# Token-column norm sums with a spread factor, and four reorderings taken back, in a three-layer fp32 block kernel

## The chip, the cores and the metric

The kernel runs on one core of a Trainium2 chip. The metric is the device time of one execution in microseconds, lower is better. All data are fp32; a matrix product is made of three products of rounded halves (high times low, high times high, low times high), so that each weight block costs three passes of TensorE.

## The reference, cut to what matters

256 tokens of width 1024 and 256 context tokens go through two layers of a first kind, then one layer of a second kind. All multiplications by weights are right products with 1024-wide inputs.

```python
def rms_norm(x, g):
    return x * rsqrt(mean(x * x, -1) + 1e-6) * g

for l in range(2):                         # first_block
    sh, sc, gt = modulation(c, ada_w[l], ada_b[l])
    h  = rms_norm(x,  norm_pre[l]) * (1 + sc) + sh
    hc = rms_norm(xc, norm_pre[l]) * (1 + scc) + shc
    z, zc = h @ w_in[l], hc @ w_in[l]      # in the last layer zc: keys and values only
    # differential attention, a long convolution, a gated MLP: y_a, y_b, y_c
    out = sum(sigmoid(z_sel_i) * ((y_i * silu(z_gate_i)) @ w_branch[l][i])) @ w_out[l]
    x   = x + gt * rms_norm(out, norm_post[l])
# second block, one layer
h = rms_norm_2(x, g_mix)                   # attention heads with rotary angles cos/sin(pos * inv_freq),
...                                        # compressed keys and values, a gated FFN, a last projection
```

## The kernel before, in words

x is kept transposed, as eight feature tiles of 128 x tokens. The weights come as one stream of 364 tiles (512 KB each, 128 x 1024 floats), in the order of use. Five engines run programs that are written out by hand and meet only in semaphores; within an engine the order of the program is the order of the work.

- SyncE (line 2707) requests a tile into one of four raw buffers once DVE has split the tile four places before (for a tile of the modulation, called ada, that is used raw: once TensorE has used it).
- ACT rounds the raw tile to its high half `whi` (act_hi, line 1271), in act_tiles three tiles ahead of the tile that it evacuates. DVE subtracts it for the low half `wlo` (dve_lo, line 1813), in dve_tiles two tiles ahead. `split=False` means that an iteration does its evacuation and no split, because one was done earlier.
- TensorE takes, per tile, eight blocks of 128 x 128, each with three products into one of four PSUM banks, `G` (lines 424 to 426).

The norms: ACT squares each feature tile (line 1255), TensorE adds the squares over the partitions by a product with a constant matrix `mean_all` (128 x 128), which leaves every partition of a 128 x 256 bank with the mean of each token; ACT takes the root (line 1259), DVE the reciprocal (line 1805), 128 x 256 each, and DVE multiplies. For the norm of `out` POOL first adds up seven of the eight squares (line 2660, pe_pooled line 636).

Layer 1 of the first kind uses the tiles 132 to 135 (queries), 136 to 139 (ada), 140 to 143 (keys), then values, convolution, MLP and gates up to 191, the terms and selectors 192 to 215 (the sum over the branches), and w_out 216 to 223. The second block begins with 224 and 225 (called zc), 226 to 228 (heads), 229 to 232 (compressed keys); later come down (332 to 353), pproj (354, 355) and pgate (356 to 363).

- pe_cross (from line 801) is the start of layer 1: the sums of the norm of x, three ada tiles, the four query tiles (pe_cross_queries, line 764, in the order QUAD, which has two or three tiles interleaved block by block as the halves of h arrive), and the fourth ada tile, 139, behind the sixth step of that order. ACT's read of the ada sums is line 1402; it stands in act_beside, ahead of h(4).
- w_out: in iteration o of eight, each engine does one tile. DVE also works out a part of the arguments of the rotary angles in o = 0 to 3 (dve_trig, line 2064: cosine in two parts, sine in two parts), and ACT applies Sin at o = 2 and 4 (line 1648). At o = 5 ACT makes a root of one column, which loads its Sqrt table early (line 1645).
- Behind w_out: the norm of out (on PE, `("out", 1)`), then eight stages x = x + factor * out (lines 2435 and 2436, semaphore x_new), each followed by ACT's square for the norm `("res", 1)`. DVE makes one extra split ahead of the first and one behind the last, ACT one rounding behind the root.
- POOL waits for x_new(1, 7), then issues the copies head_spread, ck_w2, cv_w2 (lines 2686 to 2688), because their place is in use until then. pe_block2 (line 1131) waits for the three, then for the factor of the norm, and begins with pe_mix_quad (line 1017), in which the tiles 224 to 227 are interleaved in the order QUAD as the halves hn(k) arrive.
- In the down loop DVE and POOL add the results to x and the squares for the next norm; DVE splits tile 356 in its iteration i == 4.

Of the kernel before, what the change touches and what calls it, by code (L numbers as in the profile page):

```python
# [10 lines left out]
ACT = mybir.ActivationFunctionType  # L11
# [215 lines left out]
class Kernel:  # L227
# [407 lines left out]

    def pe_pooled(self, stage, n):

        bank = self.sum_bank.get(stage, self.M[0])[:, 0:n]
# [125 lines left out]
    def pe_cross_queries(self, tiles, last_ada):  # L764

        n = 0
        for step, (i, k) in enumerate(QUAD):
# [10 lines left out]
            if step == 5:  # L778
                self.pe_tile(last_ada)
# [20 lines left out]
    def pe_cross(self):  # L800
# [4 lines left out]
        for T in moving[:3]:  # L805
            self.pe_tile(T)
        self.pe_cross_queries(queries, moving[3])
# [163 lines left out]
    def pe_block1(self, l):  # L971
# [35 lines left out]
        self.pe.wait_ge(*self.at("rstd", ("out", l)))  # L1007
        for k in range(KT):
            self.pe_sum(("res", l), k, n)
# [6 lines left out]

    def pe_mix_quad(self):

        pe, n = self.pe, 0
        tiles = self.tiles[self.pe_next:self.pe_next + 4]  # L1020
        for i, k in QUAD:
            T = tiles[i]
            s, c = T.t % SPLIT, slice(k * P, (k + 1) * P)
            if k == 0:
                pe.wait_ge(*self.at("tile_lo", T.t))
                self.pe_bank(T.use)
            if k == n:
                pe.wait_ge(*self.at("hn", "g_mix", k))
                n += 1
            m = self.three(self.G[T.use % 4][:, 0:TOK], self.whi[:, s, c], self.wlo[:, s, c], self.hi(k, 0), self.lo(k, 0), k == 0, k == KT - 1)  # L1030
            if k == KT - 1:
                m.then_inc(*self.mark("tile_used", "used", T.t))
        self.pe_next += 4
# [97 lines left out]
    def pe_block2(self):  # L1131
# [5 lines left out]
        pe.wait_ge(*self.at("rstd", ("res", 1)))  # L1137
        self.pe_mix_quad()
        self.pe_tiles(1)
        self.pe_head(0)  # L1140
        self.pe_head(1)
# [481 lines left out]
    def act_block1(self, l):  # L1623
# [16 lines left out]
        self.act_tiles(32 if l else 44)  # L1640
        act.wait_ge(*self.at("evac", self.tiles[self.act_done - 1].use))
        self.act_merged(l, KT - 1, n)
        for o in range(KT):
            if o == 5:
                act.activation(self.stat[:, 38:39], self.c["eps"], ACT.Sqrt, bias=self.c["zero"])
            if l and o in (2, 4):
                act.wait_ge(*self.at("trig_arg", o // 2 - 1))
                act.activation((self.cos, self.sin)[o // 2 - 1], self.tmp[:, 3, 0:TOK], ACT.Sin).then_inc(*self.mark("act_filter", "trig", o // 2 - 1))
# [8 lines left out]
        self.act_root(("out", l), n)  # L1657
        self.act_hi()
# [1272 lines left out]
```

## Time and profile before

| | |
|---|---|
| median of 3 runs | 1422.38 us (1420.55 to 1424.69) |
| the profiled execution | 1422.8 us, of which 1421.5 us are the span of the trace |
| mean granted TensorE clock | 0.989 of full speed |
| TensorE (PE) busy | 1373.3 us, 97% |
| VectorE (DVE) busy | 938.1 us, 66% |
| ScalarE (ACT) busy | 687.2 us, 48% |
| GpSimd (POOL) busy | 42.2 us, 3% |
| read from memory | 199.8 MB, 141 GB/s over the span |
| chain that ended last | PE 89%, DVE 6%, ACT 2%, DMA 1% |

The profile is of one execution. Times count from the start of the span; an operation is named by its engine, its line and the tiles that it writes and reads. "Idle before" is time in which the engine had nothing to run, with what released it. The 1.3 us between the execution's time and its span lie outside of the trace. Windows are stretches of the span, here the term stage (862.3 to 919.9), w_out (919.9 to 949.1) and most of the second block; (x) counts instructions. PEclk is the granted clock of TensorE, 1.00 being 2.4 GHz and 0.50 being 1.2 GHz.

### The profile page before, as it was taken

How to read it: one execution, taken by the hardware profiler on the slowest of the kernel's cores; microseconds unless marked ns; L12 is line 12 of the kernel's file. 1: busy time of each engine (PE TensorE's matmuls, PEld its weight loads, DVE VectorE, ACT ScalarE, POOL GpSimd, SP SyncE). 2: the span in 40 equal slices, each digit the busy share in tenths (PEclk: the TensorE clock that was granted, in tenths of full speed). 3: DMA queues.
4: the chain of work that ended last, by engine and by line, in shares of the span. 5: the costliest groups of instructions: out<-in, count | busy, mean ns of one | idle time of the engine just before them, and what ended most of it. 6: DMA issues, size and time to landing. Idle time of an engine off the chain costs nothing.

```text
span 1421.5 us, 20880 instructions
## 1 busy us (share of the span) xinstructions
PE 1373.3 (97%) x8316; PEld 1158.4 (81%) x8316; DVE 938.1 (66%) x1688; ACT 687.2 (48%) x1190; POOL 42.2 (3%) x50
## 2 busy tenths in 40 slices
PE   6999999999999999989999999978999999999998
PEld 3676678878888888759889999967879899888878
DVE  6565766876323334477785887686867777888456
ACT  5424554144322232554565554555657746666435
POOL 0000000000000000100000000010000002000010
PEclk9999999999999999999999999998999999999999
DMA  9431352253332332423344455543643345655542
GB/s 365 161 111 65 135 195 71 70 189 120 104 104 89 102 106 97 160 92 105 107 132 144 162 177 193 178 134 114 207 144 103 110 159 179 201 187 191 196 148 85
DMA packets 57937, 202.21 MB, mean 142 GB/s; under 512 B 6288, under 2 KB 9680, under 8 KB 57840
## 3 DMA queue, kind: packets, MB, share of 16 engines
q1 hardware_dynamic: 55712, 194.27, 40.6%
q0 software_dynamic: 1760, 6.12, 1.3%
q8 instruction: 66, 1.08, 0.3%
q10 hardware_dynamic: 368, 0.48, 0.1%
q14 instruction: 31, 0.25, 0.1%
HBM read 199.80 MB, written 1.05 MB: 141 GB/s over the span
## 4 chain that ended last, share of the span: by engine, by line
PE 89%; DVE 6%; ACT 2%; DMA 1%; issue 1%; SPq 0%; POOL 0%; ACTq 0%; DVEq 0%
PE gemm_bank L424 17%; PE gemm_bank L426 17%; PE gemm_bank L425 17%; PE misc_bank L424 4%; PE misc_bank L426 4%; PE misc_bank L425 4%; PE misc_bank L435 3%; PE gemm_bank L435 3%; PE misc_bank L835 2%; PE gemm_bank L580 1%; PE misc_bank L580 1%; PE misc_bank L436 1%; PE gemm_bank L436 1%; PE gemm_bank L513 1%; PE misc_bank L878 1%; DVE wlo L1813 1%
## 5 line engine op out<-in xcount | busy, mean ns | idle before, releaser
L1813 DVE TENSOR_TENSOR wlo<-raw,whi 128x1024 fp32r<-128x1024 f32 x316 | 382.5, 1221 | 78.1 <-ACT whi L1271 78.0
L1271 ACT ACTIVATE whi<-raw 128x1024 fp32r<-128x1024 f32 x316 | 332.5, 1055 | 181.8 <-PE gemm_bank L426 117.1
L424 PE MATMUL gemm_bank<-halves,wlo 128*128 128x256 f32 (+1 forms) x1152 | 372.9, 324 | 11.3 <-DMA shared<-in_cv_w 3.9
L426 PE MATMUL gemm_bank<-halves,whi 128*128 128x256 f32 (+1 forms) x1152 | 358.8, 311 | 0.0
L425 PE MATMUL gemm_bank<-halves,whi 128*128 128x256 f32 (+1 forms) x1152 | 358.6, 311 | 0.0
L424 PEld LDWEIGHTS gemm_bank<-halves,wlo 128*128 128x128 f32 x1152 | 221.2, 192 | 37.0 <-issue 19.0
L426 PEld LDWEIGHTS gemm_bank<-halves,whi 128*128 128x128 f32 x1152 | 221.2, 192 | 12.1
L425 PEld LDWEIGHTS gemm_bank<-halves,whi 128*128 128x128 f32 x1152 | 221.6, 192 | 11.2 <-issue 0.7
L424 PE MATMUL gemm_bank<-arena_r,wlo 128*128 128x512 f32 (+1 forms) x320 | 108.4, 339 | 4.9 <-DVE wlo L1813 4.9
L425 PE MATMUL gemm_bank<-arena_r,whi 128*128 128x512 f32 (+1 forms) x320 | 107.5, 336 | 0.0
L426 PE MATMUL gemm_bank<-arena_r,whi 128*128 128x512 f32 (+1 forms) x320 | 107.5, 336 | 0.0
L424 PE MATMUL misc_bank<-halves,wlo 128*128 128x512 f32 (+1 forms) x288 | 101.9, 354 | 0.0
L425 PE MATMUL misc_bank<-halves,whi 128*128 128x512 f32 (+1 forms) x288 | 101.9, 354 | 0.0
L426 PE MATMUL misc_bank<-halves,whi 128*128 128x512 f32 (+1 forms) x288 | 101.9, 354 | 0.0
L1848 DVE SCALAR_TENSOR_TENSOR tmp<-tmp,gemm_bank 128x512 f32<-128x512 f32 (+1 forms) x28 | 16.1, 574 | 96.2 <-ACT tmp L1340 96.2
L1340 ACT ACTIVATE tmp<-misc_bank 128x512 f32<-128x512 f32 (+1 forms) x36 | 18.9, 526 | 115.9 <-PE misc_bank L426 115.9
L424 PEld LDWEIGHTS gemm_bank<-arena_r,wlo 128*128 128x128 f32 x320 | 60.7, 190 | 14.1 <-DVE wlo L1813 6.6
L426 PEld LDWEIGHTS gemm_bank<-arena_r,whi 128*128 128x128 f32 x320 | 60.7, 190 | 6.3
L425 PEld LDWEIGHTS gemm_bank<-arena_r,whi 128*128 128x128 f32 x320 | 60.7, 190 | 6.2
L435 PE MATMUL gemm_bank<-halves,whi 128*128 128x512 f32 x176 | 62.2, 395 | 0.0
L435 PE MATMUL misc_bank<-halves,whi 128*128 128x512 f32 x176 | 62.1, 394 | 0.0
L425 PEld LDWEIGHTS misc_bank<-halves,whi 128*128 128x128 f32 x288 | 54.5, 189 | 7.5
(420 smaller groups left out, 2266.8 us busy)
## 6 DMA issues: line engine op xcount, KB each, us to landing
raw<-in_stream SPq DMA_DIRECT2D x348, 512.0 KB, 3.3
arena<-in_stream SPq DMA_DIRECT2D x16, 512.0 KB, 12.9
x<-in_x SPq DMA_DIRECT2D x1, 1024.0 KB, 6.7
x<-in_ctx SPq DMA_DIRECT2D x1, 1024.0 KB, 9.4
y<-in_hy_decay POOLq DMA_DIRECT2D x2, 512.0 KB, 4.8
arena<-in_gm_ws POOLq DMA_DIRECT2D x2, 512.0 KB, 5.8
const_b<-in_const_b POOLq DMA_DIRECT2D x1, 635.0 KB, 6.8
y<-in_hy_w POOLq DMA_DIRECT2D x2, 256.0 KB, 3.8
```

The lines of the kernel that those rows point to most:

```text
L424: mm(out, w_lo, r_hi, start=first, stop=False)
L425: mm(out, w_hi, r_lo, start=False, stop=False)
L426: return mm(out, w_hi, r_hi, start=False, stop=last)
L435: self.pe.matmul(bank[:, :], hi[:, c], self.hi_lo(k, s), start=(k == 0), stop=False)
L436: m = self.pe.matmul(bank[:, 0:TOK], lo[:, c], self.hi(k, s), start=False, stop=(k == KT - 1))
L513: m = pe.matmul(bank[c:c + 32, :], self.cond_w[:, 2 * q + kk, :], raw[:, kk * BR:(kk + 1) * BR], start=(q < 2), stop=(q >= 2), tile_positi ...
L580: pe.matmul(self.out_banks[o][:, :], hi[:, c], self.ah_al[:, j, :], start=(j == 0), stop=False)
L835: mm = pe.matmul(self.M[m][:, 0:nkeys], self.Q[r, h, q], self.K[r, h, k_off:k_off + nkeys], start=True, stop=True)
L1271: act.activation(self.whi[:, t % SPLIT, :], self.raw_tile(t), ACT.Copy).then_inc(*self.mark("tile_hi", "tile_hi", t))
L1340: act.activation(self.tmp[:, e % 2, 0:n], self.M[e][:, 0:n], ACT.Tanh, scale=0.5).then_inc(*self.mark("act_sel", "sel_tanh", T.use))
L1813: dve.tensor_tensor(self.wlo[:, t % SPLIT, :], self.raw_tile(t), self.whi[:, t % SPLIT, :].bitcast(F32), ALU.subtract).then_inc(*self.mark ...
L1848: self.own(dve.scalar_tensor_tensor(th, th, 1.0, b[:, 0:n], ALU.add, ALU.mult))
```

## The change

- The norms of `out` and of x behind it (`res`) in layer 1 have their sums as token columns: the squares are the stationary operand (one block of 128 tokens at a time), one column of `mean_all` is the moving one, and the result is 128 tokens x 1, one column for each half of the tokens. Root and reciprocal work on 128 x 2. Two products, of that column repeated 128 times with the identity matrix, spread the factors over all partitions, into the second half of the same PSUM bank, where DVE reads them.
- Tile 139 is used with the other three ada tiles, ahead of the queries.
- pe_mix_quad is gone: 224 and 225, then the heads, are used tile by tile.
- The parts of the rotary arguments stand in the term stage, behind DVE's tiles 193, 195, 203 and 205, and ACT's Sin behind its tiles 199 and 207. The early Sqrt load of layer 1 is at o == 1.
- The extra splits in the norms, and their counterparts with split=False, are gone. Tile 356 is split ahead of the down loop.

```diff
@@ new functions, ahead of pe_pooled @@
+    def token_bank(self, stage):
+        return {("out", 1): self.M[0], ("res", 1): self.M[2]}[stage]
...
+    def pe_token_sum(self, stage, squares, first, last):
+
+        for h in range(2):
+            m = self.pe.matmul(self.token_column(stage, h), squares[:, h * P:(h + 1) * P], self.c["mean_all"][:, 0:1], start=first and h == 0, stop=last and h == 1)
+        return m
+
+    def pe_token_factor(self, stage):
+
+        self.pe.wait_ge(*self.at("token_r", stage))
+        for h in range(2):
+            m = self.pe.matmul(self.token_factor(stage)[:, h * P:(h + 1) * P], self.token_stat(stage)[:, h:h + 1].broadcast_to([P, P]), self.c["ident"], start=True, stop=True)
+        m.then_inc(*self.mark("pe_sum", "rstd", stage))
+
+    def act_token_root(self, stage):
+
+        self.act.wait_ge(*self.at("summed", stage, KT - 1))
+        self.act.activation(self.token_stat(stage), self.token_bank(stage)[:, 0:2], ACT.Sqrt, bias=self.c["eps"]).then_inc(*self.mark("act_root", "root", stage))
+
+    def dve_token_rstd(self, stage):
+
+        r = self.token_stat(stage)
+        self.dve.wait_ge(*self.at("root", stage))
+        self.dve.reciprocal(r, r).then_inc(*self.mark("dve_rstd", "token_r", stage))
+        self.dve.wait_ge(*self.at("rstd", stage))
+
@@ pe_pooled @@
+        if stage == ("out", 1):
+            self.pe.wait_ge(*self.at("pooled", stage, KT - 2))
+            self.pe_token_sum(stage, self.sq_sum[:, 0:n], True, False)
+            self.pe.wait_ge(*self.at("sq", stage, KT - 1))
+            self.pe_token_sum(stage, self.tmp[:, (KT - 1) % 2, 0:n], False, True).then_inc(*self.mark("pe_sum", "summed", stage, KT - 1))
+            return
@@ pe_cross_queries, pe_cross @@
-            if step == 5:
-                self.pe_tile(last_ada)
...
-        for T in moving[:3]:
+        for T in moving:
             self.pe_tile(T)
-        self.pe_cross_queries(queries, moving[3])
+        self.pe_cross_queries(queries)
@@ pe_block1, layer 1 @@
-        self.pe.wait_ge(*self.at("rstd", ("out", l)))
+        self.pe_token_factor(("out", l))
         for k in range(KT):
-            self.pe_sum(("res", l), k, n)
+            self.pe.wait_ge(*self.at("sq", ("res", l), k))
+            self.pe_token_sum(("res", l), self.tmp[:, k % 2, 0:n], k == 0, k == KT - 1).then_inc(*self.mark("pe_sum", "summed", ("res", l), k))
@@ pe_mix_quad removed; pe_block2 @@
         pe.wait_ge(*self.landed("cv_w2"))
-        pe.wait_ge(*self.at("rstd", ("res", 1)))
-        self.pe_mix_quad()
-        self.pe_tiles(1)
-        self.pe_head(0)
-        self.pe_head(1)
+        self.pe_token_factor(("res", 1))
+        self.pe_tiles(2)
+        self.pe_heads(3)
         self.pe_tiles(4)
@@ act_block1 @@
-        self.act_tiles(32 if l else 44)
+        if l:
+            for i, n_tiles in enumerate((16, 8)):
+                self.act_tiles(n_tiles)
+                act.wait_ge(*self.at("trig_arg", i))
+                act.activation((self.cos, self.sin)[i], self.tmp[:, 3, 0:TOK], ACT.Sin).then_inc(*self.mark("act_filter", "trig", i))
+        self.act_tiles(8 if l else 44)
...
-            if o == 5:
+            if o == 5 - 4 * l:
                 act.activation(self.stat[:, 38:39], self.c["eps"], ACT.Sqrt, bias=self.c["zero"])
-            if l and o in (2, 4):
-                act.wait_ge(*self.at("trig_arg", o // 2 - 1))
-                act.activation((self.cos, self.sin)[o // 2 - 1], self.tmp[:, 3, 0:TOK], ACT.Sin).then_inc(*self.mark("act_filter", "trig", o // 2 - 1))
...
-        self.act_root(("out", l), n)
-        self.act_hi()
+        self.act_token_root(("out", l))
@@ act_block2 @@
-        self.act_root(("res", 1), TOK)
+        self.act_token_root(("res", 1))
...
-        self.act_tiles(1, split=False)
-        self.act_tiles(1)
+        self.act_tiles(2)
@@ dve_hn: token factor in PSUM for g_mix, tmp slot 2 for the others @@
+        if gain == "g_mix":
+            self.dve_token_rstd(("res", 1))
+            factor = self.token_factor(("res", 1))
@@ dve_block1 @@
-        self.dve_tiles(30 if l else 42)
+        if l:
+            for n_tiles, i, part in ((8, 0, 0), (2, 0, 1), (8, 1, 0), (2, 1, 1)):
+                self.dve_tiles(n_tiles)
+                self.dve_trig(i, part)
+        self.dve_tiles(10 if l else 42)
...
-            elif l and o < 4:
-                self.dve_trig(o // 2, o % 2)
...
-        self.dve_lo()
-        self.dve_rstd(("out", l), n)
+        self.dve_token_rstd(("out", l))
         for k in range(KT):
             out = self.branch_out(k, 0)
-            self.own(v.tensor_tensor(out, out, self.tmp[:, 2, 0:n], ALU.mult))
+            self.own(v.tensor_tensor(out, out, self.token_factor(("out", l)), ALU.mult))
             v.tensor_tensor(self.x[:, k, 0:n], self.x[:, k, 0:n], out, ALU.add).then_inc(*self.mark("dve_x", "x_new", l, k))
-        self.dve_lo()
@@ dve_block2 @@
-        self.dve_tiles(1, split=False)
-        self.dve_tiles(1)
+        self.dve_tiles(2)
         self.dve_compress("k")
-        self.dve_tiles(1, split=False)
-        self.dve_tiles(2 + 4 + 1)
+        self.dve_tiles(3 + 4 + 1)
...
         v.wait_ge(*self.at("used", self.dve_done - 1))
+        self.dve_tiles(1)
         for i in range(KT + 1):
-            if i == 4:
-                self.dve_tiles(1)
```

## Rows read from the trace of the kernel before

**Rows 1.** Part 1 of the page: busy time, share of the span, instructions.

```profile
PE 1373.3 (97%) x8316; PEld 1158.4 (81%) x8316; DVE 938.1 (66%) x1688; ACT 687.2 (48%) x1190; POOL 42.2 (3%) x50
```

**Rows 2.** Windows: length; PE, PEld, DVE, ACT, POOL busy; PEclk; DMA share; GB/s.

```profile
862.30:919.90 57.60, 57.60 (x483) 57.60 (x482) 37.93 (x58) 26.04 (x37) 0.00 (x0) 1.00 0.56 184
919.90:949.10 29.20, 24.25 (x194) 23.23 (x192) 24.56 (x48) 16.90 (x30) 5.95 (x6) 1.00 0.40 129
1008.00:1377.00 369.00, 365.05 (x2541) 327.18 (x2540) 271.45 (x548) 215.90 (x399) 8.98 (x6) 1.00 0.51 169
```

**Rows 3.** Timeline of PE, cross queries: start, length, operation, [idle before <-releaser].

```profile
620.56 1.91 PE L513 MATMUL gemm_bank<-raw,cond_w 128*32 128x512 f32 x12
...
624.72 0.36 PE L424 MATMUL gemm_bank<-halves,wlo 128*128 128x256 f32 x1 [2.25 <-DVE halves L2363]
...
628.06 1.92 PE L513 MATMUL gemm_bank<-raw,cond_w 128*32 128x512 f32 x4
...
640.42 0.70 PE L762 MATMUL misc_bank<-tmp,const_a 128*128 128x256 f32 x2 [1.69 <-ACT tmp L1584]
```

**Rows 4.** Windows, around tile 139 in the cross queries.

```profile
626.50:630.00 3.50, 3.50 (x14) 1.61 (x12) 0.84 (x3) 0.00 (x0) 0.00 (x0) 0.51 0.46 181
```

**Rows 5.** Timeline of SP: the request of tile 139.

```profile
620.59 0.33 SPq L2707 DMA_DIRECT2D raw<-in_stream  x1
```

**Rows 6.** Part 6 of the page: issues, KB each, median us to landing.

```profile
raw<-in_stream SPq DMA_DIRECT2D x348, 512.0 KB, 3.3
```

**Rows 7.** Timeline of ACT, cross queries.

```profile
630.03 0.60 ACT L1402 ACTIVATE const_a<-gemm_bank 128x512 f32<-128x512 f32 x1 [3.73 <-PE gemm_bank L513]
```

**Rows 8.** Waits from 919 to 950: waiter <- releaser: total, times, longest.

```profile
PE gemm_bank L424 <- DVE wlo L1813: 4.9, 3, 2.5
```

**Rows 9.** Windows: the first trig part in wout.

```profile
923.35:926.85 3.50, 3.50 (x31) 3.50 (x31) 3.23 (x10) 2.40 (x6) 0.43 (x1) 1.00 0.46 150
```

**Rows 10.** Timelines of DVE and PE: the split of tile 197, its first product.

```profile
860.28 1.22 DVE L1813 TENSOR_TENSOR wlo<-raw,whi 128x1024 fp32r<-128x1024 f32 x1
...
865.16 0.28 PE L424 MATMUL gemm_bank<-arena_r,wlo 128*128 128x256 f32 x1
```

**Rows 11.** Source view, L1431: min/median/max ns, starts, forms.

```profile
L1431 ACT ACTIVATE hy_rs<-misc_bank,const_a x2: 263/263/263, 75.8 to 611.4; 128x4 f32<-128x4 f32 x2
L1431 ACT ACT_TABLE_LOAD  x1: 1283/1283/1283, 74.5 to 74.5; - x1
```

**Rows 12.** Timeline of ACT: the last square of out.

```profile
949.77 0.39 ACT L1255 ACTIVATE tmp<-gemm_bank 128x256 f32<-128x256 f32 x1
```

**Rows 13.** Timeline of DVE: the reciprocal of out.

```profile
951.81 1.75 DVE L1805 RECIPROCAL tmp<-tmp 128x256 f32<-128x256 f32 x1 [0.65 <-ACT tmp L1259]
```

**Rows 14.** Timeline of PE: small fp32 products, one column and 128 columns.

```profile
610.42 0.95 PE L694 MATMUL misc_bank<-const_a,arena 128*128 128x1 f32 x8
...
769.71 2.34 PE L902 MATMUL misc_bank<-tmp,const_a 128*128 128x128 f32 x16
```

**Rows 15.** Source view, L2096.

```profile
L2096 DVE RECIPROCAL stat<-stat x24: 158/166/168, 121.6 to 751.1; 128x2 f32<-128x2 f32 x24
```

**Rows 16.** Chain of work behind x_new(7): start, us, what.

```profile
959.62 0.44 DVE x L2436
...
961.41 4.29 DMA shared<-in_cv_w
```

**Rows 17.** Timeline of DVE: two of the eight hn stages.

```profile
965.60 0.48 DVE L2334 SCALAR_TENSOR_TENSOR tmp<-x,const_b,tmp 128x256 f32<-128x256 f32 x1
...
966.33 0.48 DVE L2334 SCALAR_TENSOR_TENSOR tmp<-x,const_b,tmp 128x256 f32<-128x256 f32 x1
```

**Rows 18.** Timeline of PE: tile 231.

```profile
989.44 0.30 PE L424 MATMUL gemm_bank<-whi,cmp_xl 128*30 128x256 f32 x1 [0.88 <-DVE wlo L1813]
```

**Rows 19.** Timeline of DVE: the split of tile 356.

```profile
1382.52 1.75 DVE L1813 TENSOR_TENSOR wlo<-raw,whi 128x1024 fp32r<-128x1024 f32 x1
```

**Rows 20.** Timeline of PE: the fourth pproj group.

```profile
1384.65 0.58 PE L424 MATMUL misc_bank<-arena_r,wlo 128*128 128x256 f32 x1 [1.29 <-DVE tmp L2628]
```

More of the change, by code:

```diff
@@ L634, in pe_sum, with token_column, token_factor, token_stat @@
         self.pe.matmul(self.sum_bank.get(stage, self.M[0])[:, 0:n], self.c["mean_all"], self.tmp[:, k % 2, 0:n], start=first, stop=last).then_inc(*self.mark("pe_sum", "summed", stage, k))
-    def pe_pooled(self, stage, n):
+    def token_bank(self, stage):
+        return {("out", 1): self.M[0], ("res", 1): self.M[2]}[stage]
+    def token_column(self, stage, h):
+        return self.token_bank(stage)[:, h:h + 1]
+    def token_factor(self, stage):
+        return self.token_bank(stage)[:, TOK:ALL]
+    def token_stat(self, stage):
+        c = {("out", 1): 34, ("res", 1): 36}[stage]
+        return self.stat[:, c:c + 2]
+    def pe_token_sum(self, stage, squares, first, last):
[15 more added lines that the diff above has]
+        self.dve.wait_ge(*self.at("rstd", stage))
+    def pe_pooled(self, stage, n):
+        if stage == ("out", 1):
[4 more added lines that the diff above has]
+            return
         bank = self.sum_bank.get(stage, self.M[0])[:, 0:n]
@@ L762, in pe_cross_sum, with pe_cross_queries @@
         self.pe.matmul(self.M[0][:, self.half(s)], self.c["mean_all"], self.tmp[:, k % 2, self.half(s)], start=(k == 0), stop=(k == KT - 1)).then_inc(*self.mark("pe_sum", "summed", ("res", 0, s), k))
-    def pe_cross_queries(self, tiles, last_ada):
+    def pe_cross_queries(self, tiles):
         n = 0
@@ L1015, in pe_head @@
         pe.matmul(self.M[0][:, 0:TOK], self.c["head_win"][:, 26 - 2 * n:26 - 2 * n + P], self.tmp[:, 0, (n % 2) * TOK:(n % 2 + 1) * TOK], start=(n == 0), stop=(n == 13)).then_inc(*self.mark("pe_head", "head_ms", n))
[L1017 to L1033, printed above, removed]
     def pe_heads(self, count):
@@ L2329, in dve_hn @@
         v, slots = self.dve, (0, 1, 3, 4)
-        self.dve_rstd({"g_mix": ("res", 1)}.get(gain, gain), TOK)
+        if gain == "g_mix":
+            self.dve_token_rstd(("res", 1))
+            factor = self.token_factor(("res", 1))
+        else:
+            self.dve_rstd(gain, TOK)
+            factor = self.tmp[:, 2, 0:TOK]
         for k in range(KT + 1):
@@ L2333, in dve_hn @@
                 t = self.tmp[:, slots[k % 4], 0:TOK]
-                v.scalar_tensor_tensor(t, self.x[:, k, 0:TOK], self.c[gain][:, k:k + 1], self.tmp[:, 2, 0:TOK], ALU.mult, ALU.mult).then_inc(*self.mark("dve_h", "hn_sum", gain, k))
+                v.scalar_tensor_tensor(t, self.x[:, k, 0:TOK], self.c[gain][:, k:k + 1], factor, ALU.mult, ALU.mult).then_inc(*self.mark("dve_h", "hn_sum", gain, k))
             if k:
```

## The prediction

> **What bounds the kernel now.** I read the busy times first: TensorE (PE) has 97% of the span [rows 1]. The windows then say where it is solid: 365.05 us of the 369 from 1008 to 1377 are PE work at granted clock 1.00, and the 57.60 of the term/sel stage are full to the last digit [rows 2]. In such a stretch a faster DVE or ACT earns nothing, but an added DVE step can cost. PE's idle time lies in four places, and the change touches each: the cross queries (622 to 641), the wout stretch (919.9 to 949.1), the two norms behind it (949 to 966, then tiles 225 to 231), and the tail behind 1377. So I go place by place and ask what comes last there, before and after. A gain in one place passes whole to the end, because what follows is PE-bound.
>
> **Cross queries: tile 139 back with the other three.** The queries (tiles 132 to 135) cannot start before 624.72, where PE waits 2.25 for the DVE's first halves [rows 3]. PE is free from 622.5. Tile 139, an ada tile used raw, costs 1.92 at clock 0.51, and runs at 628.06, amid the queries [rows 3, 4]. At full clock it is .64 (its three sisters ahead took 1.91 together [rows 3]) to .98 (1.92 times .51); I take .86, between, in the idle 2.25. Can it be there in time? Its raw buffer is requested at 620.59 [rows 5]; a raw tile lands in 3.3 [rows 6], so 623.9, done by 624.7: it just fits. Moved with it: ACT's read of its sum (L1402), which waited 3.73 for it and stood ahead of h(4) to h(7) [rows 7]. ACT and then DVE get on earlier by 2.96: the low half of h(4) moves from 631.06 to some 628.1. The reciprocal, x_new(1) and its square follow, and so PE's wait of 1.69 at 640.42 [rows 3] ends earlier by as much. PE's own work from 624.7 shrinks by the 1.9 of the tile, and 1.69 of idle time goes, so PE allows more than 2.96; DVE's chain decides. I take **2.9**, bounds 1.0 (the tile lands late, a wait in front of all queries, with SP's request behind the split of tile 135) and 3.0.
>
> **Trig out of the wout loop.** Today 29.2 us [rows 2] hold 192 products at .119, that is 22.9, and .2 of edges: 6.0 are lost. 4.9 of it are three waits of PE for a split tile [rows 8], which DVE delivers late because of the four trig parts (3.50, 3.35, 3.50, 3.05: 13.4 in all; the first is shown [rows 9]). Without them DVE has 24.56 less 13.4 [rows 2], 11.2 of work, in the 23 us: all 6.0 come back.
> The parts now stand behind tiles 193, 195, 203 and 205, in a stage where DVE is busy 37.93 of 57.60 [rows 2], so 19.7 are free, .98 for each of 20 tiles, against 13.4. That covers the sum, not each piece. A split is done some 3.7 before PE wants it (that of tile 197 ends at 861.50, PE starts it at 865.16 [rows 10]). A part of 3.5 eats this lead; two tiles later 2.0 are won back; the next part finds 2.3 and misses 1.1, and behind it the split of tile 196's successor waits for a bank that DVE's own late evacuation frees, .6 more. By a schedule written out so: .25 + 1.72 for the first pair, .38 + .40 for the second (eight tiles between them restore the lead), **2.75**. Bounds: 0 (slack takes it) and 13.4 (all bare). I take 2.75, since the lead has a row. ACT's two Sin and their table loads (1.28 each [rows 11], four in all) go along; ACT is busy 26.04 of 57.60 [rows 2] and rounds 3 tiles ahead, so they are hidden; without that cover 5.1. Net **3.25**.
> The Sqrt preload moves from o = 5 to o = 1: hidden too, ACT waits there.
>
> **Norm of out as token columns.** Before: the wout products end at 949.1 [rows 2], the last square starts only at 949.77, behind a rounding [rows 12]; the reciprocal runs from 951.81 for 1.75 [rows 13], and the first multiply follows at 953.59: 4.5. After, from the rows nearest: square .45; its two products of one column, and the wait for their tail, .58 (8 such in .95 [rows 14]: 4 records are .44, .14 over); root on 128x2 .28 (a 128x4 took .263 [rows 11]); reciprocal .17 (128x2 [rows 15]); factor, 2 fp32 products of 128 columns as 4 records, .6 (16 took 2.34 [rows 14], .11 a step and .28 for the last); hand-overs between four engines .17. That is 2.25, **gain 2.25**, bounds 1.5 and 2.9 (a hand-over may cost 0.0 or 0.2 more at each of five). The eight x stages stay at .80 each; DVE's multiply reads PSUM now; I cost that at nothing (0 to .5 for all eight). The square of the last tile no longer stands behind a rounding; that rounding is simply later, with 5 us of slack behind the norm.
>
> **Norm of res, and the mix quad.** Let N be the end of x_new(7), 960.06 before [rows 16]. The token sums, root and reciprocal are through about N+2, which would be 2.2 ahead of the old reciprocal's end (N+4.2). But the factor product stands in pe_block2 behind the wait for cv_w2, whose copy can only be issued behind x_new(7): 1.35 of issue and two POOL steps, then the transfer of 4.29, from 961.41 [rows 16], and .2: over at N+5.86. So the factor comes at N+6.4; three DVE and ACT steps of .4 to .5 give the first pair of halves 1.4 on, and zc0 starts at N+8.0; DVE hands one k each .73 (start to start [rows 17]), so zc0 is paced by it and ends N+13.3; the quad, in the old order, had up to four tiles' work for each k from N+5.86 on, though with the clock low (about .5, as in [rows 4]). From there four tiles of 2.88 bring PE to the compress tile 229 at N+26.1, old N+25.7. There the old run waits for splits, the last .88 at 989.44 [rows 18], whose DVE stream is .7 earlier in the new order: PE resumes tile 231 at N+29.05, old N+29.40. A gain of .1, and .4 since no weight transfer runs beside cv_w2 now (before, one was issued at 961.2): **.5**, bounds -1.5 (clock at its lower level of 1.2 GHz for more of zc0 to head0) and +1.2. The shorter norm is thus worth nothing in this place: the transfer covers it, and if it were gone the gain would be 3.5. The removed splits ahead (in both norms) return as one split each behind; DVE has 10 us of stall here, so they are hidden.
>
> **Split of tile 356.** It took 1.75 in the down loop, next to POOL's adds, and PE waited 1.29 for DVE's sum at 1384.65 [rows 19, 20]. Ahead of the loop it costs 1.22 (its like: [rows 10]), of which .68 delays the first add, and PE's fourth pproj group starts 1.0 earlier. **1.0**, bounds -.7 (the delayed first add runs through the loop) and 1.3.
>
> **Sum.** 2.9 + 3.25 + 2.25 + .5 + 1.0 = 9.9. The profiled run took 1422.8 (span 1421.5 and 1.3 around it): 1412.9. The median of the runs is .4 lower: **1412.5**.
>
> **Rivals.** (A) Trig stalls the term stage more: PE is solid there and a bank freed late, a part slowed by work beside it (a split of 1.22 once took 1.75 [rows 19]) or by ACT's Sin, which waits for the parts, doubles or triples the 2.75. For: a part of 3.5 takes nearly the whole lead. Against: 19.7 of slack. 5.5 to 8.3 lost instead: 1415.3 to 1418. (B) The cross order gains nothing, since tile 139 lands after 624.7 and holds the queries by about what it saves (or the edit doesn't do what it says: ACT's read is then still last), with trig at 5.7 to 8.4 or the res part at its bound of -1.5: 1412.5 + 2.9 + 2.9 = 1418.3, up to 1422.4. For: the landing leaves .0 to .8. Against: h(0) alone sets 624.72 today. (C) Slower: all four parts bare (13.4) and the four table loads ahead of roundings too (5.1): 18.5 instead of 2.75, 1428.3. It decides once the term stage loses over 12.6, the whole of the other gains. For it DVE would have to miss its lead at each part in full; 37.93 busy of 57.60 speaks against.
> The Trainium skill (ScalarE: Activation LUTs, What ACT_TABLE_LOAD costs) puts a switch at about 1283 ns of load and 1380 ns of drain, 2.66 us; an estimate by it is 10.6 for four, which would help C; the row has the load at its 1283 ns, and an ACTIVATE some 20 ns behind, without a drain.
>
> **How the numbers follow.** Forecast with its bounds .67; A .15; B .12; C .06. A comparison can tell some 0.3% (4.3 us) here from no change: faster means under 1418.1, forecast and A, .82; B is within, .12; C is slower, .06. From the bounds the forecast's own range is 1408.5 (2.4 of trig hidden, res +1.2, tail and out norm at their best: 4 more) to about 1416. For 8 in 10 A must be in and the start of B: 1408.5 to 1419.0.
>
> **What would show it.** Cross: tile 139's products ahead of the queries at full clock, the wait of 3.73 gone, PE's first sum of the next norm 2.9 earlier. Term stage: 60.3 long in place of 57.6, with PE waits on splits of tiles 196 to 198 and 206 to 208; wout 23.1. Out norm: 2.3 from last product to first multiply. Res: factor directly behind the landing of cv_w2, first mix product 2 us later against x_new(7) than before, tile 231 at the same distance. Tail: no wait over .3 at the fourth pproj group. I am wrong if the term stage is over 63, if ACT's read of tile 139 still waits over 1, or if tiles 225 to 231 stay at the lower clock.

## The result and the profile after

The changed kernel takes 1411.6 us (median of 4 runs, 1410.05 to 1414.5), the kernel before 1421.47 in the same comparison (1420.25 to 1424.69); the ratio is 0.9929, 95% interval 0.9906 to 0.9953. The prediction was 1412.5, faster. The profiled execution of the changed kernel is the slowest of its four (1414.5, span 1413.2), which has to be kept in mind below: 1.7 us of that is a later start, and about 1.1 a stretch of low clock that lies late.

Part 1 of the page of the changed kernel, and three windows of its trace (columns as in [rows 2]):

```profile
PE 1372.9 (97%) x8344; PEld 1163.3 (82%) x8344; DVE 932.3 (66%) x1688; ACT 691.4 (49%) x1193; POOL 41.1 (3%) x50
```

```profile
861.10:920.10 59.00, 57.16 (x472) 56.59 (x471) 46.66 (x85) 31.35 (x43) 0.00 (x0) 1.00 0.58 187
920.10:944.10 24.00, 24.00 (x203) 24.00 (x201) 11.95 (x13) 16.14 (x28) 5.15 (x6) 1.00 0.61 199
949.50:966.60 17.10, 12.53 (x55) 12.09 (x55) 10.89 (x28) 7.37 (x19) 2.13 (x4) 0.50 0.13 37
```

PE's busy time is the same to .4 us (1373.3 before [rows 1]); all of the gain is idle time. The w_out stretch is full now (24.00 of 24.00; 24.25 of 29.20 before [rows 2]) and the term stage no longer is (57.16 of 59.00). The third window is new: 17.1 us in one piece at granted clock 0.50, that is 1.2 GHz, through the x stages and the first mix tile. Before, the clock fell there twice, for 6.8 us each (at 954.19 and 964.43).

To see where time goes, follow one and the same instruction through both traces and subtract. Each step of the difference belongs to the stage in between:

| instruction | before | after | difference | stage's share |
|---|---|---|---|---|
| first ada product | 620.56 | 622.25 | +1.69 | start, +1.69 |
| PE's second sum after the queries | 640.42 | 638.30 | -2.12 | cross queries, -3.81 |
| a product of tile 208 | 896.97 | 897.81 | +0.84 | trig in the term stage, +2.96 |
| first product of tile 223 | 943.06 | 938.03 | -5.03 | w_out, -5.87 |
| first multiply by the factor of out | 953.59 | 946.33 | -7.26 | norm of out, -2.23 |
| product behind the splits of 229 to 232 | 1005.05 | 997.51 | -7.54 | norm of res and mix, -0.28 |
| last product of the down loop | 1377.06 | 1369.51 | -7.55 | 370 us of solid PE, -0.01 |
| first pproj group | 1378.44 | 1371.53 | -6.91 | DVE's first add, behind the split of 356, +0.64 |
| fourth pproj group | 1384.65 | 1376.26 | -8.39 | no split in the down loop, -1.48 |
| span | 1421.5 | 1413.2 | -8.3 | rest, +0.09 |

The start (+1.69) is not the change's: up to here all kernels are the same program, and at this point the traces of the twelve experiments lie between 0.9 earlier and 1.1 later than that of the kernel before. Without it the shares sum to -10.0, close to the medians (-9.9). The two rows on tile 356 belong together: the split ahead of the down loop makes PE wait 1.74 for DVE's first add in place of 1.09, and the fourth group gets 1.48 back, so the edit is worth 0.84 there.

One share is an accident of this trace. From the first product of tile 223 to the product of 997.51 the changed kernel takes 59.48 (before: 61.99). The kernels u1, u4 and v2 below run the same instructions there and take 58.41, 58.29 and 58.36. Their stretch at clock 0.50 is as long (17.1), but begins 9.2 to 9.8 behind the first product of tile 223, and that of the changed kernel 11.5 behind it, so that it reaches further into the mix. By those three traces the share of the norm of res and the mix is some -1.4, not -0.28. Where an experiment is compared at 997.51 below, I give u4_split_old beside the changed kernel for this reason.

### The profile page after: what moved, and what is told of

Read it like the earlier page. It is cut to its first block, busy times and chain, and to the rows that moved or that the text cites. A ratio compares the mean times of both kernels' runs of the same rounds, so it can differ in the third digit from the quotient of the medians.

```text
span 1413.2 us, 20938 instructions
## 1 busy us (share of the span) xinstructions
PE 1372.9 (97%) x8344; PEld 1163.3 (82%) x8344; DVE 932.3 (66%) x1688; ACT 691.4 (49%) x1193; POOL 41.1 (3%) x50
## 3 DMA queue, kind: packets, MB, share of 16 engines
HBM read 199.80 MB, written 1.05 MB: 142 GB/s over the span
## 4 chain that ended last, share of the span: by engine, by line
PE 88%; DVE 7%; DMA 2%; ACT 2%; issue 1%; POOL 0%; ACTq 0%; SPq 0%; DVEq 0%
PE gemm_bank L424 17%; PE gemm_bank L426 17%; PE gemm_bank L425 17%; PE misc_bank L424 4%; PE misc_bank L426 4%; PE misc_bank L425 4%; PE misc_bank L435 3%; PE gemm_bank L435 3%; PE misc_bank L877 2%; PE gemm_bank L580 1%; PE misc_bank L580 1%; PE misc_bank L436 1%; PE gemm_bank L436 1%; PE gemm_bank L513 1%; DMA raw<-in_stream 1%; PE misc_bank L920 1%
## 5 line engine op out<-in xcount | busy, mean ns | idle before, releaser
L1294 ACT ACTIVATE whi<-raw 128x1024 fp32r<-128x1024 f32 x316 | 332.7, 1055 | 184.5 <-PE gemm_bank L426 116.3
L424 PEld LDWEIGHTS misc_bank<-halves,wlo 128*128 128x128 f32 x288 | 54.5, 189 | 8.2 <-DVE wlo L1836 0.8
```

The lines of the kernel that those rows point to most:

```text
L424: mm(out, w_lo, r_hi, start=first, stop=False)
L1294: act.activation(self.whi[:, t % SPLIT, :], self.raw_tile(t), ACT.Copy).then_inc(*self.mark("tile_hi", "tile_hi", t))
```

## The experiments

All are edits of the changed kernel. "Against the changed kernel" is the difference of the two ratios to the kernel before, times 1422. Single runs of one kernel spread by 1 to 6 us, and the changed kernel's own interval is 3.3 us to either side. So only u5, v3 and v4 differ from it clearly by the times, v2 and v5 barely; for the others the trace, not the time, carries the argument.

| kernel | median | ratio to before (95%) | against the changed kernel |
|---|---|---|---|
| changed | 1411.60 | 0.9929 (0.9906 to 0.9953) | |
| u1_cross_old | 1414.33 | 0.9944 (0.9932 to 0.9955) | +2.1 |
| u2_trig_old | 1415.89 | 0.9951 (0.9939 to 0.9963) | +3.1 |
| u3_out_old | 1412.29 | 0.9933 (0.9921 to 0.9945) | +0.6 |
| u4_split_old | 1412.24 | 0.9931 (0.9919 to 0.9943) | +0.3 |
| u5_quad | 1418.15 | 0.9974 (0.9965 to 0.9983) | +6.4 |
| u6_res_old | 1408.50 | 0.9910 (0.9895 to 0.9925) | -2.7 |
| u7_quad_splits | 1415.49 | 0.9944 (0.9932 to 0.9956) | +2.1 |
| v1_late_waits | 1410.84 | 0.9920 (0.9906 to 0.9934) | -1.3 |
| v2_trig_spread | 1407.82 | 0.9902 (0.9889 to 0.9916) | -3.8 |
| v3_late_spread | 1406.34 | 0.9882 (0.9869 to 0.9895) | -6.7 |
| v4_res_old_spread | 1405.19 | 0.9876 (0.9863 to 0.9889) | -7.5 |
| v5_all_orders | 1409.04 | 0.9903 (0.9889 to 0.9916) | -3.7 |

### The cross order undone

```diff
                 m.then_inc(*self.mark("tile_used", "used", T.t))
+            if step == 5:
+                self.pe_tile(last_ada)
...
-        for T in moving:
+        for T in moving[:3]:
```

> The changed kernel with tile 139 put back behind the sixth step of the queries. My theory (DVE's chain of h was held up by ACT's read of tile 139, and PE's own 1.9 us at half clock lay amid the queries): the stretch from the first ada product to PE's second sum of the res norm is 3.0 to 3.8 us longer, ACT waits over 3 us at the read of the ada sums, and the time is about 3.5 over the changed kernel, some 1415. Rival (the late landing of tile 139, for which PE waits 1.42 in the changed kernel, eats what the order brings): not over 1.5 longer.

The timelines of ACT and PE of this kernel show both waits of [rows 3] and [rows 7] again:

```profile
628.85 0.60 ACT L1427 ACTIVATE const_a<-gemm_bank 128x512 f32<-128x512 f32 x1 [3.44 <-PE gemm_bank L513]
...
639.23 0.70 PE L806 MATMUL misc_bank<-tmp,const_a 128*128 128x256 f32 x2 [1.69 <-ACT tmp L1609]
```

From the first ada product to PE's second sum it takes 19.55, against 16.05 in the changed kernel: 3.5 longer, as my theory had it (the medians show 2.1, within their noise). In the changed kernel the same places read (timelines of PE and ACT):

```profile
622.25 1.91 PE L513 MATMUL gemm_bank<-raw,cond_w 128*32 128x512 f32 x12
625.58 1.05 PE L513 MATMUL gemm_bank<-raw,cond_w 128*32 128x512 f32 x4 [1.42 <-DMA raw<-in_stream]
...
638.30 0.70 PE L806 MATMUL misc_bank<-tmp,const_a 128*128 128x256 f32 x2 [0.72 <-ACT tmp L1607]
```

```profile
627.90 0.58 ACT L1425 ACTIVATE const_a<-gemm_bank 128x512 f32<-128x512 f32 x1
```

PE does wait for the landing of tile 139, but in time that was idle anyway; ACT's read now starts without a wait.

### The trig parts back in w_out

```diff
-            for n_tiles, i, part in ((8, 0, 0), (2, 0, 1), (8, 1, 0), (2, 1, 1)):
-                self.dve_tiles(n_tiles)
-                self.dve_trig(i, part)
...
+            elif l and o < 4:
+                self.dve_trig(o // 2, o % 2)
```

> The changed kernel with the trig parts and both Sin back in the w_out loop. My theory (6 us of wout were DVE's delay of the splits, and 3.0 of it are paid again in the term stage): term stage 57.6 us without a wait of PE, w_out stretch 29 instead of 24, together 2.9 longer: some 1414.5. Rival (the stalls in the term stage have another cause than the trig parts, such as the landing of raw tiles): the waits at tiles 198 and 206 stay, and the time grows by the full 5.9, to 1417.5.

Waits of PE (waiter <- releaser: total, times, longest), first of the changed kernel from 856 to 945, then of this one from 850 to 950, and two windows of this one, the term stage and w_out:

```profile
PE gemm_bank L424 <- DVE y L1884: 1.5, 1, 1.5
PE misc_bank L424 <- DVE wlo L1836: 0.3, 1, 0.3
```

```profile
PE gemm_bank L424 <- DVE wlo L1834: 3.9, 2, 2.6
...
PE misc_bank L652 <- POOL sq_sum L2681: 0.8, 1, 0.8
```

```profile
860.00:917.50 57.50, 57.50 (x482) 57.50 (x481) 37.45 (x58) 25.67 (x38) 0.00 (x0) 1.00 0.54 179
917.50:946.20 28.70, 23.98 (x182) 23.31 (x181) 24.01 (x46) 17.21 (x30) 7.22 (x6) 0.94 0.43 141
```

The term stage is full again, so its stalls are the trig parts' alone; the rival, landings, falls. The term stage gives 2.94 back. Up to the first product of tile 223 the w_out loop then takes 6.04 more (5.9 expected): the waits for splits are 3.9 here (4.9 in [rows 8]), and the clock fell to 0.50 for 3.4 us, which cost 1.5. Up to PE's first sum of the norm of out it is 7.04, since POOL's last add takes 1.51 beside DVE's splits (0.74 in the changed kernel, where DVE is idle) and holds that sum by 0.8. Some 1.4 of it is given back behind the norms, mostly by the late stretch of the changed kernel's trace.

### The norm of out on 128 x 256 again

```diff
-        self.act_token_root(("out", l))
+        self.act_root(("out", l), n)
...
-        self.dve_token_rstd(("out", l))
+        self.dve_rstd(("out", l), n)
```

> The changed kernel with the norm of out on 128 x 256 again (sum by mean_all, root, reciprocal, factor in SBUF), the res norm left on token columns. My theory: the last product of w_out to the first multiply takes 2.0 to 2.3 longer than in the changed kernel (4.3 to 4.6), the x stages keep .80 each, all later work shifts by that: some 1413.8. Rival (a small root and reciprocal only move the wait, because POOL's pooled sum comes last): less than .7 longer.

Timelines of ACT and DVE of this kernel, then of ACT, DVE and PE of the changed one, from the last square to the first multiply:

```profile
942.28 0.38 ACT L1272 ACTIVATE tmp<-gemm_bank 128x256 f32<-128x256 f32 x1 [1.09 <-PE gemm_bank L426]
...
943.96 1.75 DVE L1822 RECIPROCAL tmp<-tmp 128x256 f32<-128x256 f32 x1 [4.39 <-ACT tmp L1276]
945.74 0.42 DVE L2458 TENSOR_TENSOR halves_f<-halves_f,tmp 128x256 f32<-128x256 f32 x1
```

```profile
943.99 0.38 ACT L1278 ACTIVATE tmp<-gemm_bank 128x256 f32<-128x256 f32 x1 [1.09 <-PE gemm_bank L426]
...
945.07 0.26 ACT L665 ACTIVATE stat<-misc_bank,const_a 128x2 f32<-128x2 f32 x1 [0.24 <-PE misc_bank L652]
...
945.36 0.17 DVE L671 RECIPROCAL stat<-stat 128x2 f32<-128x2 f32 x1 [4.08 <-ACT stat L665]
946.33 0.42 DVE L2464 TENSOR_TENSOR halves_f<-halves_f,misc_bank 128x256 f32<-128x256 f32 x1 [0.80 <-PE misc_bank L659]
```

3.46 against 2.34: the token columns alone are worth 1.12, not 2.2. The missed expectation is instructive. Before, it took 3.82 from the last square [rows 12] to the first multiply, and the square itself started .7 behind the last product, since a rounding stood ahead of it. That .7, and POOL's slow adds (its last one ended at 950.08, only then could PE sum), went with the trig parts and the extra rounding, both of which this experiment leaves away. Against the changed kernel's trace even the 1.12 seems gone at 997.51, but that is the accident named above: the stretch at clock 0.50 is here 2.0 earlier against the first product of tile 223. In u4_split_old it lies within 0.2 of the same place, and against that trace this kernel takes 1.35 longer up to this product (59.64 against 58.29). So the 1.12 lasts; the time (+0.6) is too coarse to tell.

Its profiled run also shows an event that comes and goes between runs. Windows of it at the attention scores of the second block:

```profile
1048.20:1051.60 3.40, 3.40 (x27) 2.91 (x26) 1.16 (x4) 2.34 (x2) 0.00 (x0) 1.00 0.51 160
1051.60:1058.40 6.80, 6.80 (x32) 5.67 (x32) 5.88 (x22) 1.92 (x4) 0.00 (x0) 0.50 0.42 134
```

The clock fell for 6.8 us there, which cost 2.9 (PE stands 1.55 ahead of the changed kernel in front of it and 1.37 behind it after it). The same fall is in the trace of u7_quad_splits at 1054.4, and in none of before, after or the others. Such falls may be what makes single times of one kernel differ by 2 to 5 us; with one trace of each kernel this is not shown.

### The split of tile 356 undone

```diff
-        self.dve_tiles(1)
         for i in range(KT + 1):
+            if i == 4:
+                self.dve_tiles(1)
```

> The changed kernel with the split of tile 356 back in iteration 4 of the down loop. My theory (this split, at 1.75 beside POOL's adds, was PE's wait of 1.29): the wait for DVE's sum at the fourth pproj group is back and the stretch from 3 us ahead of the down loop's end to the first head product of the next norm is 1.0 to 1.5 longer: some 1412.9. Rival (clock level in the tail, which fell at 1380.9 before and at 1372.8 after, made the difference): no change beyond .5.

Timelines of DVE and PE of this kernel, then of DVE and PE of the changed one, then of PE of the kernel before:

```profile
1373.07 1.74 DVE L1836 TENSOR_TENSOR wlo<-raw,whi 128x1024 fp32r<-128x1024 f32 x1
...
1375.20 0.39 PE L424 MATMUL misc_bank<-arena_r,wlo 128*128 128x256 f32 x1 [1.95 <-DVE tmp L2654]
```

```profile
1369.83 1.22 DVE L1836 TENSOR_TENSOR wlo<-raw,whi 128x1024 fp32r<-128x1024 f32 x1 [3.27 <-PE misc_bank L581]
1370.97 0.42 DVE L2653 TENSOR_TENSOR tmp<-misc_bank,tmp 128x256 f32<-128x256 f32 x1
...
1371.53 0.35 PE L424 MATMUL misc_bank<-arena_r,wlo 128*128 128x256 f32 x1 [1.74 <-DVE tmp L2653]
...
1376.26 0.41 PE L424 MATMUL misc_bank<-arena_r,wlo 128*128 128x256 f32 x1
```

```profile
1378.44 0.36 PE L424 MATMUL misc_bank<-arena_r,wlo 128*128 128x256 f32 x1 [1.09 <-DVE tmp L2628]
```

The split has a price in either place: in the down loop PE waits for the fourth sum, ahead of it for the first. Counted from the last product of the down loop, the fourth group starts 7.58 later here and 6.75 later in the changed kernel: 0.83 lost, not 1.0 to 1.5. But the clock of the changed kernel fell at 1372.78 for 6.8 us (products of 0.41 us), and that of this one didn't (0.39 and less). So at the next group, the first behind the sums of the next norm, this kernel is even 0.33 ahead (9.84 against 10.17), which is the rival's "no change beyond .5". Six other traces take out the clock: u2, u3, v1, v2, v3 and v4 have the changed kernel's instructions here without the fall, and all take 8.8 to that group. So the fall costs 1.35, and at equal clock the split is worth 1.0 (9.84 against 8.8, both without a fall) or 0.8 (10.95 before against 10.17, both with one). The time says +0.3, within noise.

### The quad, alone and with the splits that belonged to it

```diff
-        self.pe_tiles(2)
-        self.pe_heads(3)
+        self.pe_mix_quad()
+        self.pe_tiles(1)
+        self.pe_head(0)
+        self.pe_head(1)
```

> The changed kernel with pe_mix_quad back (224 to 227 interleaved, waits in place, token columns kept). My theory (at this point PE is held by DVE's hn, .73 for each k, which at the clock's lower level is little more than one tile's .64 of products, so interleaving fills little): tile 231 starts 0 to 1.0 earlier in the quad order, time 1411 to 1412. Rival (the quad gives work for each hn and its loss cost 2 to 3 us, hidden by the shorter norm): 1409.

```profile
965.00 0.39 PE L424 MATMUL gemm_bank<-halves,wlo 128*128 128x256 f32 x1 [1.77 <-DVE wlo L1856]
...
978.08 0.58 PE L424 MATMUL gemm_bank<-halves,wlo 128*128 128x256 f32 x1 [3.47 <-DVE wlo L1856]
```

Neither theory foresaw 6.4 us. PE's timeline names it: the quad needs tiles 226 and 227 split early, and the extra splits that provided this are gone; with the second stall comes another stretch of 6.8 us at clock 0.50. So the experiment had undone half of a pair. The next one undoes both:

```diff
         self.act_token_root(("out", l))
+        self.act_hi()
...
+        self.dve_lo()
         self.dve_token_rstd(("out", l))
```

> The changed kernel with the quad and the extra splits of both norms back (the order of before), token columns kept, waits in place. My theory (the quad alone lost 5 us because tiles 226 and 227 were not split when it came to them, waits of 1.8 and 3.5 for DVE; with the splits ahead it is what before had): those two waits are gone, tile 231 within 1 us of the changed kernel, time 1411 to 1412.5. Rival (the quad is bad with a factor that comes at the landing, whatever the splits): 1415 or more.

Waits of PE in this kernel from 945 to 1003, and in the changed kernel from 945 to 1002:

```profile
PE misc_bank L659 <- DMA shared<-in_cv_w: 3.7, 1, 3.7
PE gemm_bank L424 <- DVE wlo L1858: 2.1, 2, 1.2
...
PE misc_bank L1058 <- ACT tmp L1401: 1.5, 2, 1.0
```

```profile
PE misc_bank L659 <- DMA shared<-in_cv_w: 3.0, 1, 3.0
PE gemm_bank L424 <- DVE wlo L1836: 2.0, 2, 1.2
```

The stalls of 1.77 and 3.47 are gone, and 2.2 us stay against the changed kernel (at the factor product of out this kernel is .63 ahead, at the product of 997.51 it is 1.60 behind). 1.5 of them are two waits of the head sums for ACT: the quad finishes four tiles at almost the same time, so that the squares of the first two heads queue up. Tile by tile these are spread. The other 0.8 is the copy cv_w2, which took 3.94 in place of 3.16: with the extra splits a weight tile is requested right ahead of the copies again (953.27), as before the change. The expected "within 1 us" was too low, and the rival's 1415 came nearer.

### The res norm, and what stands behind the copies

```diff
-        self.pe_token_factor(("res", 1))
+        pe.wait_ge(*self.at("rstd", ("res", 1)))
...
-            factor = self.token_factor(("res", 1))
+            factor = self.tmp[:, 2, 0:TOK]
```

> The changed kernel with the res norm on 128 x 256 again (its sum in a bank of its own), the rest as changed, waits in place. My theory (the landing of cv_w2 at N + 4.5 to 5.9 covers the old norm, whose reciprocal ended N + 4.2): the first mix product is up to 1.7 EARLIER than in the changed kernel, since no factor product (1.2 at half clock) and no hn pair stand behind the landing: some 1410. Rival (the token form of res is what gained 2 us here): first mix product 1.5 or more later, 1413.

The chain of work (start, us, what) of the changed kernel, then of this one:

```profile
952.32 0.44 DVE x L2465
...
954.11 3.16 DMA shared<-in_cv_w
957.26 0.25 issue
957.51 1.21 PE misc_bank L659 x4
...
958.74 0.49 DVE tmp L2362
...
960.28 0.55 PE gemm_bank L424
```

```profile
948.67 3.92 PE misc_bank L634 x10
...
952.62 0.48 ACT tmp L1281
...
953.12 1.76 DVE tmp L1827
...
956.45 0.55 PE gemm_bank L424
```

The old form never waits for the copy: root, reciprocal and the first hn pair run while it lands. In the changed kernel 1.21 of factor product at the lower clock and 1.5 of hn stand behind the landing. Against the end of x_new(7) the first mix product is 1.8 earlier in the old form (5.76 behind it, 7.53 in the changed kernel). At 997.51 the old form is 2.0 ahead of the changed kernel and 0.8 ahead of u4_split_old. The time goes down by 2.7, but 1.2 of that in the trace lies in the down loop, where the two are the same program (u1's trace gains as much there). The token form of this norm is a loss as it stands, of about 1 to 2 us.

The other cure is to keep the token form and to wait for the copies only where they are read:

```diff
-        pe.wait_ge(*self.landed("cv_w2"))
         self.pe_token_factor(("res", 1))
...
+        pe.wait_ge(*self.landed("cv_w2"))
         pe.wait_ge(*self.at("hid2", "k"))
```

> The changed kernel with the waits for head_spread, ck_w2 and cv_w2 moved from ahead of the factor of the res norm to the first product that reads ck_w2, some 30 us later. My theory (the shorter res norm is worth nothing because the factor stands behind the landing of cv_w2): the factor product starts 3.0 earlier against x_new(7), the mix tiles follow, and at tile 231 2.5 to 3.0 of it are left: some 1409. Rival (DVE's stream of splits or the lower clock sets tiles 229 to 232, so the earlier start turns into waits there): less than 1 is left at tile 232, 1411.

```profile
954.32 1.22 PE L659 MATMUL misc_bank<-const_a,stat 128*128 128x128 f32 x4 [0.55 <-DVE stat L671]
957.12 0.55 PE L424 MATMUL gemm_bank<-halves,wlo 128*128 128x256 f32 x1 [1.57 <-DVE halves L2366]
```

The factor (in PE's timeline) now waits for the reciprocal and starts 2.3 earlier against x_new(7) (2.45 behind it, 4.77 in the changed kernel), not 3.0. At the product of 997.51 this kernel is 3.3 ahead of the changed kernel's trace, but only 2.1 ahead of u4_split_old; v3 against v2, below, gives 2.2 there too. So some 2.2 is left, less than the 2.5 to 3.0 that I expected. The time shows 1.3: three of its six runs lie near 1408.4 and three at 1412.5, with mean clocks of 0.991 to 0.994 and of 0.990. I read this as the coming and going fall of the clock; it isn't shown, as those runs have no trace.

### Placing the trig parts by the stage's slack, and the sums of edits

```diff
-            for n_tiles, i, part in ((8, 0, 0), (2, 0, 1), (8, 1, 0), (2, 1, 1)):
+            for n_tiles, i, part in ((13, 0, 0), (3, 0, 1), (6, 1, 0), (3, 1, 1)):
```

> The changed kernel with the four trig parts 3, 6 and 3 tiles apart (behind DVE's tiles 198, 201, 207, 210), each ahead of one of the stage's idle times of 2.2 to 2.6 us of DVE, and the two Sin behind ACT's tiles 203 and 211. My theory (the 2.9 us of stall in the term stage come from a second part that finds the lead not won back, and from the tiles 194 to 197, whose evacuation leaves DVE almost no slack): at most .5 of PE waits is left in the term stage, 2.5 less than in the changed kernel, some 1409. Rival (the table loads and Sin on ACT, or DVE's total, stall the stage wherever the parts stand): 2 or more stay.

Window of the term stage of this kernel:

```profile
857.90:915.50 57.60, 57.60 (x482) 57.60 (x481) 48.96 (x93) 31.79 (x43) 0.00 (x0) 1.00 0.54 177
```

DVE is busy 48.96 of 57.60 and PE isn't idle at all. The same 13.4 us of work cost 6 in w_out, 3 in the changed kernel's places, and nothing here. The rival (ACT's table loads) falls with it.

v3 has this and the late waits together:

> Trig parts spread and the waits for the three copies moved behind the mix: both edits alone took 3.8 and .8 to 3 us. If they add, as places far apart in a PE-bound kernel should: 3 us under v2 in the trace, 1405 (1404.5 to 1407). Rival (the gain of the late waits is lost in a lower clock behind it, as in half of its runs): 1407.

It came out at 1406.34: 2.8 below v2 by the ratios and 2.2 ahead of it in the trace at 997.51, as much as the late waits gave alone, so they add. v4 has the spread parts and the res norm of u6:

> Trig parts spread, the res norm on 128 x 256, waits in place. If they add: 1407.8 less 3.1, 1404.7. My theory of why the token form of res costs: with the wait ahead of the factor, the factor product and the first hn pair (2.8 in all) stand behind the landing, and only the reciprocal of 1.75 ahead of it is saved; so the first mix product stands 1.6 closer to x_new(7) than in the changed kernel. Against v3: some .5 to 1 later at the first mix product, so equal or up to 1 slower.

1405.19, the fastest of all: 1.24% under the kernel before (interval 1.11 to 1.37). Its lead over v3, 0.8 by the ratios, is within noise; in the traces it is 0.3 at the product of 997.51. The first mix product did not come later than in v3, as I had expected, but a little earlier: 5.07 behind x_new(7), against 5.25. Its windows, from the norm of out to the mix, show what helped; the last wide sums of the norm fall into the one at full clock:

```profile
942.80:946.20 3.40, 3.04 (x7) 1.97 (x8) 3.23 (x10) 1.56 (x4) 0.00 (x0) 0.50 0.00 0
946.20:953.00 6.80, 3.06 (x10) 1.26 (x9) 4.86 (x9) 2.90 (x7) 2.14 (x4) 1.00 0.32 92
953.00:956.40 3.40, 3.14 (x13) 3.13 (x14) 3.40 (x11) 1.72 (x5) 0.00 (x0) 0.50 0.02 5
```

6.8 us at the lower clock in two pieces, against 13.7 in one in v3 and 17.1 in the changed kernel. v5 is v3 with quad and extra splits:

> v3 with the quad and the extra splits of both norms: the mix has all four tiles' work for each hn, and their splits are ready. My theory (PE at the lower clock has .64 of work in one tile against DVE's .73 per k; once at full clock it waits): 0 to 1.5 under v3. Rival (the extra splits stand ahead of the first multiply and in front of hn, on DVE's chain): 1 to 2 slower than v3.

3.0 us slower than v3 by the ratios, 1.9 of it at the product of 997.51; its trace also has a fall of the clock in the tail, which v3's has not. The same waits of the head sums for ACT (.51 and .98) and for tile 231's split (.88) are in its trace. So it went the rival's way, and by its amount, but not for its reason: the first mix product stands 2.8 behind the factor product in both. The quad loses here too, where no factor waits for the landing.

## Why the prediction was right, point by point

- **Cross queries, 2.9: 3.8 in the trace, 3.5 undone (u1).** Mechanism right. Tile 139 took 1.05 rather than .86 and landed 1.42 after PE was free, so the queries start .15 later than before against the first ada product (4.31 behind it, 4.16 before). The mis-sized term is ACT's read, which I let delay the chain: its .58 fit into ACT's idle time of .28 per k, so the h chain came 3.8 earlier and not 2.96.
- **Trig in the term stage, 2.75: 2.96.** Piece by piece too: .25, 1.72, .38 and .40 were written out, the trace has .37, 1.70, .57 and .32 (PE's steps from start to start beyond the usual .12), and the large one is released by the evacuation (L1884), as said. The bounds 0 and 13.4 were both real possibilities; the row on the lead decided. u2 and v2 show that the price is a matter of place alone.
- **w_out, 6.0: 5.87** (6.04 in u2).
- **Norm of out, 2.25: 2.23, by luck in its parts.** 1.12 is the token form (u3); the rest is the square that no longer stands behind a rounding and POOL's adds at 0.74 in place of 1.51. I had counted the whole of it to the new form and had named only the rounding, without a number.
- **Norm of res and mix, .5: .28 in this trace, some 1.4 by u1, u4 and v2**, a little over my upper bound of 1.2. That the shorter norm is worth nothing behind the landing of cv_w2 was right, and too kind: against the old form it is a loss, 1.8 at the first mix product (u6). What pays for it is the quad's removal, 2.2 (u7), 1.9 (v5). My working had both signs (zc0 2.1 later, made good by tile 231) but laid the recovery to DVE's stream; it is mostly the head sums' waits for ACT, 1.5, which I had not seen in the trace of before. Two terms of the first mix product were mis-sized and partly cancelled: the copy took 3.16, not 4.29, and the factor product, at the lower clock, 1.21, not .54. So it came 7.53 behind x_new(7), not 8.0. The gain of 3.5 "if the transfer were gone" measures 2.2 (v1, v3).
- **Split of 356, 1.0: 0.84 at the group, 0.8 to 1.0 at equal clock.** Right in both parts: the first add was to be delayed by .68, and PE waits .65 longer for it.
- **Rivals.** A and B did not come; C was far (2.96 lost in the term stage, decision point 12.6).
- **The sum, 9.9: 9.9 by the medians.** That it fits to the tenth is luck: the interval of the ratio runs from 6.7 to 13.4 us, and the terms for the cross queries and for the mix were each some 0.9 too small.

Not settled: when the clock falls at 1051 to 1055 and in the tail, what sets the place and length of its stretch through the norms, and why the down loop ran 1.2 us faster in the traces of u1 and u6 at the same granted clock.

## What to carry to other kernels

A shortened step is worth what the latest wait behind it leaves: before a norm is made faster, look for waits between it and its users, and put them where their data is read. Work moved off a critical loop into a stage with slack wants its place chosen by the lead of the work that it delays (pieces of 3.5 us against a lead of 3.7, no closer than the slack of the tiles in between wins back), not by the stage's mean. And an order and the prefetches made for it are one edit: undone singly, each looks worse than it is.

## What the runs showed of the hardware

- A POOL add of 128 x 256 took 0.74 with DVE idle (changed) and 1.51 beside DVE's splits (before, u2); a split of 1.22 took 1.74 to 1.75 beside POOL's adds (u4, before).
- Single falls of the clock that come and go between kernels with the same instructions: 6.8 us at 0.50 cost 2.9 at the attention scores (u3, u7) and 1.35 in the tail (changed).
- Where PE had only the narrow sums of the res norm to do, its clock was low for longer. With the sums as token columns the stretch at 0.50 was 17.1 us (changed, u1 to u5, u7, v2) or 13.7 (v1, v3, v5); with sums of 128 x 256 in the res norm it was two pieces of 6.8 (u6, below, as before) or of 3.4 (v4). The mix products that fall into the stretch take .21 from start to start in place of .12. This was seen in one trace of each kernel, and the cause was not tried apart from the norms' form.

Windows of u6_res_old from the x stages to the mix:

```profile
944.80:951.60 6.80, 5.93 (x13) 3.56 (x14) 5.65 (x15) 3.10 (x8) 0.62 (x2) 0.50 0.00 0
951.60:955.10 3.50, 0.98 (x4) 0.30 (x2) 1.94 (x2) 0.70 (x2) 1.52 (x3) 0.99 0.63 174
955.10:961.90 6.80, 5.45 (x23) 5.40 (x24) 6.57 (x17) 4.41 (x11) 0.00 (x0) 0.50 0.01 4
```
